# Expert stage: gathers and spreads as float32 matmuls in place of bfloat16 and float32r parts

## The chip, the cores and the metric

The kernel runs on one core of a Trainium2 chip. The metric is the device time of one execution in microseconds (us), as the median of several runs. Engines are named as in the profile: PE is TensorE (PEld its weight loads), DVE VectorE, ACT ScalarE, POOL GpSimd, SP SyncE, which issues most transfers.

## The reference, cut to what matters

One layer on 512 tokens of width 1024: a mixer (gated spatial MLP beside windowed attention), then a mixture of 32 experts, then a norm. The change lies in the mixture:

```python
glog = xf @ w_rg + b_rg                       # 4 groups
gsel = jnp.argmax(glog, axis=-1)
elog = jnp.take_along_axis(elog_all, gsel[:, None, None], axis=1)[:, 0]   # 8 experts of the group
topv, topi = lax.top_k(elog, 2)
tw = jax.nn.softmax(topv, axis=-1) * pg
...
for e in range(N_EXPERTS):
    h = jax.nn.silu(xf @ w_gate[e]) * (xf @ w_up[e])
    y = y + combine[:, e:e + 1] * (h @ w_down[e])
```

All inputs and the output are float32. `xf` is the normed `hn`, 512 x 1024. `w_gate[e]` and `w_up[e]` are 1024 x 512, `w_down[e]` is 512 x 1024. A token goes to two experts.

## The kernel before, in words

**Mixer** (to about 466 us). Projections are split by hand into float32r halves (hi and lo) and done with three matmuls each. Two places use plain float32 matmuls: the spatial gate (L627, stationary 128x128, 128 columns moving) and the attention scores (L565, 64 rows of contraction, 128 or 192 columns moving).

**Norm and routing** (about 466 to 502 us). ACT scales `hg` by the row's norm (`scale_h`, L923). Three bfloat16 parts of the normed rows are then made, tile by tile: ACT writes `hn_part[0]` (`first_part`, L927), POOL subtracts it in place (`first_rest`, L463), ACT writes `hn_part[1]` (`second_part`, L931), POOL subtracts again into `hn_part[2]` (`third_part`, L469). Beside it DVE computes the routing, a chain of small dependent instructions: the inverse root of the norm (L1004 to L1010), the group softmax's argument (L1268, for which ACT does an exponential at L946), the two best experts (L1261 to L1265), the softmax of two (L1284), and each token's row among the gathered rows. `make_onehot(i)` (L1306 to L1313) turns these into two weighted matrices for pair i, their sum `weight_a`, and the bfloat16 `onehot` (1 where the sum is over 0).

**Experts** (about 502 to 1017 us). A loop over 16 pairs of experts; each expert of a pair has 64 rows, so that a pair fills 128 partitions. The PE's order within pair i is written out by hand in `expert_pair`:

1. gate projection (L730, 16 matmuls; each uses 64 columns of the array, the two experts by turns), transposes of `weight_a` (L741), up projection (L730);
2. gather of the next pair's rows, tiles 0 and 1 of 8 (L714), transposes of the activations (L747), gather of tiles 2 and 3;
3. down projection in two halves of 512 columns (L755);
4. spread: for each half n and token block t, `onehotT` against `y_hi` and `y_lo` (L767, L768), added to `h_tok` by DVE (L1371);
5. gather of tiles 4 to 7.

A gather of one tile is, for 4 token blocks and 3 parts, a matmul of `hn_part[j]` (stationary) by `onehot` (moving, 128 columns): 12 bfloat16 matmuls accumulating exactly the float32 rows. The result goes through PSUM banks 2 and 3 to `packT` (ACT and DVE copy one half each). For the spread DVE sums each row's weight (L1353) and makes `onehotT` in float32r (L1354); ACT writes `y_hi` (the down result times the row's weight, in float32r, L970), and DVE `y_lo`, the rest (L1364).

A float32 matmul of 128 or more columns stands in the trace as two MATMUL instructions, each with its weight load; bfloat16 and float32r matmuls stand as one.

**Order of loads.** SP streams the weights through nine 16 KB buffers W[0] to W[8] (L333, L344, L376). Each load waits for the semaphore of the projection that used the buffer before. The load into W[8], which lies over `hg`, waits for `part2_ready`. ACT's order in routing is a fixed list of copies, scalings, parts and two exponentials.

**End.** After the last addition DVE sets `h_final`; ACT, DVE and POOL do the final norm, and SP stores the result.

## Time and profile before

| | |
|---|---|
| median of 3 runs | 1037.84 us (1035.43 to 1037.91) |
| profiled execution | span 1034.2 us from its first to its last instruction; no other time is printed for it |
| PE busy | 958.9 us, 93% |
| DVE, ACT, POOL busy | 489.2, 269.6, 25.0 us |
| moved by DMA | 247 MB, mean 239 GB/s |
| mean granted PE clock | 0.975 |

Busy time of an engine is the union of its instructions. A row of the timeline gives start, length, engine, line, operation, output <- input and a count of merged instructions. A row of a group gives busy time, mean length of one instruction, and the idle time in front with what ended it. Matmuls are pipelined: one's length is more than the distance to the next, so the pace is read from groups. L12 is line 12 of the kernel.

### The profile page before, as it was taken

To read this page: it belongs to the slowest core of one execution; us is meant where nothing else is said; L and a number is where in the kernel's file an instruction comes from. 1 tells how busy PE (TensorE), PEld (TensorE's weight loads), DVE (VectorE), ACT (ScalarE), POOL (GpSimd) and SP (SyncE) were. 2 spreads that over 40 slices of the span, in tenths; PEclk is the share of its full clock that TensorE was granted. 3 is DMA by queue.
4 is the path that set the end of the run, shared out by engine and by line. 5 is a ranking of instruction groups with operands and counts; after the bars stand their busy time and mean duration, and the time that the engine had idled before them with its cause. 6 is when DMAs were issued, how large, how long until landed. Compare 5 with 4: busy or idle time off the path is not lost.

```text
span 1034.2 us, 13947 instructions
## 1 busy us (share of the span) xinstructions
PE 958.9 (93%) x5675; PEld 624.5 (60%) x5675; DVE 489.2 (47%) x918; ACT 269.6 (26%) x427; POOL 25.0 (2%) x25
## 2 busy tenths in 40 slices
PE   3999999999999999593599999999999999999993
PEld 3888888777777888482454455554545545455442
DVE  3636335766672444258643443443443424434335
ACT  5323223644442211125121112120111211121102
POOL 0000000000000000005000000000000000000001
PEclk9999999999999999897699999999999999999997
DMA  8353222122115446834297999999999979999942
GB/s 285 82 111 93 86 78 82 42 82 71 52 57 138 132 120 229 282 127 163 107 364 323 387 395 388 413 402 390 394 383 413 402 268 392 412 387 395 396 155 83
DMA packets 93268, 247.12 MB, mean 239 GB/s; under 512 B 22168, under 2 KB 45744, under 8 KB 84784
## 3 DMA queue, kind: packets, MB, share of 16 engines
q1 hardware_dynamic: 90528, 245.90, 63.6%
q10 hardware_dynamic: 2704, 0.71, 0.3%
q8 instruction: 26, 0.43, 0.2%
q14 instruction: 10, 0.08, 0.0%
HBM read 244.50 MB, written 2.10 MB: 238 GB/s over the span
## 4 chain that ended last, share of the span: by engine, by line
PE 89%; DVE 6%; issue 1%; ACTq 1%; ACT 1%; DMA 1%; SPq 0%; DVEq 0%; POOL 0%; POOLq 0%
PE bank L730 22%; PE bank L755 11%; PE bank L714 9%; PE bank L504 9%; PE bank L506 9%; PE bank L505 9%; PE bank L767 3%; PE bank L768 3%; PE bank L531 3%; PE bank L533 3%; PE bank L532 2%; PE bank L565 2%; ACTq L900 1%; PE bank L741 1%; DMA x_tok<-x 1%
## 5 line engine op out<-in xcount | busy, mean ns | idle before, releaser
L730 PE MATMUL bank<-W,packT 128*64 128x512 f32 x1024 | 226.8, 595 | 2.9 <-issue 2.9
L730 PEld LDWEIGHTS bank<-W,packT 128*64 128x64 f32 x1024 | 74.1, 137 | 132.6 <-issue 131.6
L1017 DVE TENSOR_TENSOR wlo<-raw,whi 128x2048 fp32r<-128x2048 f32 x34 | 77.7, 2288 | 100.4 <-ACT whi L805 100.3
L504 PE MATMUL bank<-xnT_hi,whi 128*128 128x512 f32 x288 | 113.7, 395 | 0.8 <-DVE wlo L1017 0.8
L755 PE MATMUL bank<-W,actT 128*64 128x512 f32 x512 | 113.4, 595 | 0.0
L506 PE MATMUL bank<-xnT_hi,wlo 128*128 128x512 f32 x288 | 112.2, 390 | 0.0
L505 PE MATMUL bank<-xnT_lo,whi 128*128 128x512 f32 x288 | 112.2, 389 | 0.0
L714 PEld LDWEIGHTS bank<-onehot,hn_part 128*128 128x128 bf16 x1632 | 95.0, 99 | 25.0 <-issue 24.8
L714 PE MATMUL bank<-onehot,hn_part 128*128 128x128 bf16 x1632 | 101.9, 222 | 7.6 <-DVE onehot L1311 7.6
L1364 DVE SCALAR_TENSOR_TENSOR y_lo<-bank,small,y_hi 128x512 fp32r<-128x512 f32 x32 | 24.0, 751 | 145.4 <-ACT y_hi L970 145.4
L805 ACT ACTIVATE whi<-raw 128x2048 fp32r<-128x2048 f32 x34 | 64.8, 1909 | 87.5 <-PE bank L506 30.2
L1371 DVE TENSOR_TENSOR h_tok<-bank,h_tok 128x512 f32<-128x512 f32 x128 | 77.8, 678 | 0.0
L755 PEld LDWEIGHTS bank<-W,actT 128*64 128x64 f32 x512 | 35.3, 137 | 65.6 <-issue 64.0
L1353 DVE TENSOR_REDUCE small<-bank 128x1 f32<-128x512 f32 x16 | 11.1, 691 | 112.9 <-PE bank L741 112.9
L504 PEld LDWEIGHTS bank<-xnT_hi,whi 128*128 128x128 f32 x288 | 54.1, 188 | 12.6 <-issue 1.4
L506 PEld LDWEIGHTS bank<-xnT_hi,wlo 128*128 128x128 f32 x288 | 54.1, 188 | 11.4
L505 PEld LDWEIGHTS bank<-xnT_lo,whi 128*128 128x128 f32 x288 | 54.1, 188 | 10.8
L767 PE MATMUL bank<-y_hi,onehotT 128*128 128x512 f32 x128 | 51.8, 405 | 0.0
L970 ACT ACTIVATE y_hi<-bank,small 128x512 fp32r<-128x512 f32 x32 | 22.0, 688 | 113.3 <-PE bank L755 113.3
L963 ACT ACTIVATE silu_g<-bank 128x512 f32<-128x512 f32 x16 | 9.6, 597 | 156.6 <-PE bank L730 156.6
L768 PE MATMUL bank<-y_lo,onehotT 128*128 128x512 f32 x128 | 50.1, 391 | 0.0
L965 ACT ACTIVATE actT<-bank 128x512 f32<-128x512 f32 x16 | 9.6, 597 | 142.7 <-PE bank L747 142.7
(231 smaller groups left out, 1193.5 us busy)
## 6 DMA issues: line engine op xcount, KB each, us to landing
W<-w_up SPq DMA_DIRECT2D x32, 2048.0 KB, 11.2
W<-w_down SPq DMA_DIRECT2D x64, 1024.0 KB, 12.6
W<-w_gate SPq DMA_DIRECT2D x30, 2048.0 KB, 12.0
raw<-w_in SPq DMA_DIRECT2D x18, 1024.0 KB, 5.1
raw<-w_in SPq DMA_DIRECT2D x16, 256.0 KB, 4.4
raw<-w_branch_a SPq DMA_DIRECT2D x4, 1024.0 KB, 4.9
raw<-w_branch_b SPq DMA_DIRECT2D x16, 256.0 KB, 4.6
raw<-w_out SPq DMA_DIRECT2D x4, 1024.0 KB, 5.1
```

The source lines that it names most:

```text
L504: pe.matmul(dst, hi_w, hi_x, start=start, stop=False)
L505: pe.matmul(dst, hi_w, lo_x, start=False, stop=False)
L506: return pe.matmul(dst, lo_w, hi_x, start=False, stop=stop)
L531: pe.matmul(dst, xT_hi[:, kk, ts], w_h[:, k, :], start=first, stop=False)
L714: mm = pe.matmul(bank[2 + c // 4][:, (c % 4) * P:(c % 4 + 1) * P], hn_part[j][:, t, c, :], onehot[:, t, :], start=(t == 0 and j == 0), sto ...
L730: mm = pe.matmul(dst[s * ROWS:(s + 1) * ROWS, :], packT[:, c, s * ROWS:(s + 1) * ROWS], W[u][:, c * DE:(c + 1) * DE], start=(c == 0), stop ...
L755: mm = pe.matmul(bank[5 + n][s * ROWS:(s + 1) * ROWS, :], actT[:, c, s * ROWS:(s + 1) * ROWS], W[4 + s][:, c * D + n * 512:c * D + (n + 1) ...
L767: pe.matmul(dst, onehotT[:, t * P:(t + 1) * P], y_hi[:, n * 512:(n + 1) * 512], start=True, stop=False)
L768: pe.matmul(dst, onehotT[:, t * P:(t + 1) * P], y_lo[:, n * 512:(n + 1) * 512], start=False, stop=True).then_inc(spread_done, 1)
L805: act.activation(whi[c % 2][:, :], raw[c % 2][:, :], ACT.Copy).then_inc(hi_split, 1)
L1017: dve.tensor_tensor(wlo[c % 2][:, :], raw[c % 2][:, :], whi[c % 2][:, :].bitcast(F32), ALU.subtract).then_inc(lo_split, 1)
L1371: dve.tensor_tensor(part, bank[SPREAD_BANKS[n][t]][:, :], part, ALU.add).then_inc(h_added, 1)
```

## The change

The three bfloat16 parts become one float32 tensor `hn`, written by `scale_h` into its own place (it no longer overwrites `hg`). `first_part`, `second_part` and POOL's eight subtractions are gone. ACT scales all four tiles before its first exponential. `onehot` becomes float32 and is moved to another address. A gather is 4 float32 matmuls a tile in place of 12 bfloat16 ones. In the spread, the weights stay in the matrix: DVE copies the transposed `weight_a` to `weightT` (float32), ACT copies the down result to `y_rows` unweighted, and one float32 matmul takes the place of two float32r ones. `row_weight`, `onehotT`, `y_hi` and `y_lo` are gone. Two waits for `part2_ready` (SP's before W[8], PE's before the first gather) become waits for `hn_ready`.

```diff
--- before.py
+++ after.py
@@ -109,12 +97,11 @@
 
 
     W = [at(f"W{u}", [P, 8 * DE], F32, kb) for u, kb in enumerate((0, 16, 32, 48, 64, 80, 160, 144, 128))]
-    hn_part = [at(f"hn_part{j}", [P, TT, KT, P], BF16, 96 + 8 * j) for j in range(3)]
+    hn = at("hn", [P, TT, KT, P], F32, 96)
     packT = at("packT", [P, KT, P], F32, 120)
-    y_hi = at("y_hi", [P, D], F32R, 124)
+    y_rows = at("y_rows", [P, D], F32, 124)
     hg = at("hg", [P, TT, KT, P], F32, 128)
     hgT = [at(f"hgT{j}", [P, KT, 2 * P], F32, 144 + 8 * j) for j in range(2)]
-    hn_rest = hg
     h_tok = at("h_tok", [P, TT, D], F32, 176)
     ffn_g = at("ffn_g", [P, D], F32, 192)
     w_router = at("w_router", [P, KT, P // 2], F32, 196)
@@ -125,11 +112,10 @@
     silu_g = at("silu_g", [P, DE], F32, 200)
     act_rows = at("act_rows", [P, FT, P], F32, 202)
     actT = at("actT", [P, FT, P], F32, 204)
-    onehot = at("onehot", [P, TT, P], BF16, 206)
+    onehot = at("onehot", [P, TT, P], F32, 192)
     weight_a = at("weight_a", [P, TT, P], F32, 214)
     weight_b = at("weight_b", [P, TT, P], F32, 216)
-    y_lo = at("y_lo", [P, D], F32R, 192)
-    onehotT = at("onehotT", [P, SEQ], F32R, 196)
+    weightT = at("weightT", [P, SEQ], F32, 196)
     row_iota = at("row_iota", [P, P], F32, 207.5)
     final_g = at("final_g", [P, D], F32, 208)
     result = at("result", [P, TT, D], F32, 32)
@@ -146,7 +132,6 @@
     ln_stats, ln_mv = col(TT * 12), col(TT * 2)
     neg_max, sink_e, denom = ([col(REP) for _ in range(2)] for _ in range(3))
     w_first, w_second, row_first, row_second = col(TT), col(TT), col(TT), col(TT)
-    row_weight = col(1)
     half_sq = ln_stats[:, 0:2 * TT]
 
     room = [208.0]
@@ -264,8 +249,6 @@
         dve_step = sem("dve_step")
         hsq_summed, hg_ready, hgT_psum, hgT_a, hgT_b, rstd_ready = (
             sem(n) for n in ("hsq_summed", "hg_ready", "hgT_psum", "hgT_a", "hgT_b", "rstd_ready"))
-        part0_ready, rest_ready, part1_ready, part2_ready = (
-            sem(n) for n in ("part0_ready", "rest_ready", "part1_ready", "part2_ready"))
         logitsT_done, logitsT_ready, logits_turned = (
             sem(n) for n in ("logitsT_done", "logitsT_ready", "logits_turned"))
         route_sub, route_exp, picked_ready, ranks_done, routed = (
@@ -276,9 +259,8 @@
         gate_half_done = sem("gate_half_done")
         gate_done, up_done, silu_ready, rows_ready, rows_turned, actT_ready = (
             sem(n) for n in ("gate_done", "up_done", "silu_ready", "rows_ready", "rows_turned", "actT_ready"))
-        y_left, y_right, y_hi_ready, y_lo_ready = (sem(n) for n in ("y_left", "y_right", "y_hi_ready", "y_lo_ready"))
-        weights_turned, row_weight_ready, onehotT_ready = (
-            sem(n) for n in ("weights_turned", "row_weight_ready", "onehotT_ready"))
+        y_left, y_right, y_ready = (sem(n) for n in ("y_left", "y_right", "y_ready"))
+        weights_turned, weightT_ready = sem("weights_turned"), sem("weightT_ready")
         spread_done, h_added = sem("spread_done"), sem("h_added")
         ysq_summed, final_gained, out_stored = sem("ysq_summed"), sem("final_gained"), sem("out_stored")
         y_rstd_ready = sem("y_rstd_ready")
@@ -372,7 +354,7 @@
             sp.wait_ge(logitsT_done, 2)
             sp.dma_start(W[7][:, :], w_gate[0, 3].rearrange("(p c) n -> p (c n)", p=P)).then_inc(w_loaded[7], 16)
 
-            sp.wait_ge(part2_ready, TT)
+            sp.wait_ge(hn_ready, TT)
             sp.dma_start(W[8][:, :], w_up[0, 2].rearrange("(p c) n -> p (c n)", p=P)).then_inc(w_loaded[8], 16)
 
             for half, used in enumerate((gate_half_done, gate_done)):
@@ -457,23 +439,6 @@
             pool.wait_ge(route_iotas_made, 6)
             pool.affine_select(out=earlier[:, :], in_=all_ones[:, :], compare_op=ALU.is_gt, fill=0.0, base=0,
                                pattern=[[1, P]], channel_multiplier=-1).then_inc(route_iotas_made, 1)
-
-            def first_rest(t):
-                pool.wait_ge(part0_ready, t + 1)
-                pool.tensor_tensor(hn_rest[:, t, :, :], hn_rest[:, t, :, :], hn_part[0][:, t, :, :],
-                                   ALU.subtract).then_inc(rest_ready, 1)
-
-            def third_part(t):
-                pool.wait_ge(rest_ready, min(t + 2, TT))
-                pool.wait_ge(part1_ready, t + 1)
-                pool.tensor_tensor(hn_part[2][:, t, :, :], hn_rest[:, t, :, :], hn_part[1][:, t, :, :],
-                                   ALU.subtract).then_inc(part2_ready, 1)
-
-            first_rest(0)
-            for t in range(1, TT):
-                first_rest(t)
-                third_part(t - 1)
-            third_part(TT - 1)
 
             pool.wait_ge(late_loaded, 16 * 6)
             pool.wait_ge(h_final, 1)
@@ -710,10 +675,8 @@
                     if c == 0:
                         pe.wait_ge(onehot_ready, i + 1)
                     for t in range(TT):
-                        for j in range(3):
-                            mm = pe.matmul(bank[2 + c // 4][:, (c % 4) * P:(c % 4 + 1) * P],
-                                           hn_part[j][:, t, c, :], onehot[:, t, :],
-                                           start=(t == 0 and j == 0), stop=(t == TT - 1 and j == 2))
+                        mm = pe.matmul(bank[2 + c // 4][:, (c % 4) * P:(c % 4 + 1) * P], hn[:, t, c, :], onehot[:, t, :],
+                                       start=(t == 0), stop=(t == TT - 1))
                     if c % 4 == 3:
                         mm.then_inc(pack_done, 1)
 
@@ -757,20 +720,18 @@
                                            start=(c == 0), stop=(c == FT - 1))
                     mm.then_inc(done, 1)
 
-                pe.wait_ge(onehotT_ready, i + 1)
+                pe.wait_ge(weightT_ready, i + 1)
                 for n in range(2):
-                    pe.wait_ge(y_lo_ready, 2 * i + n + 1)
+                    pe.wait_ge(y_ready, 2 * i + n + 1)
                     for t in range(TT):
                         if n == 1 and t >= 2:
                             pe.wait_ge(h_added, 8 * i + t - 1)
-                        dst = bank[SPREAD_BANKS[n][t]][:, :]
-                        pe.matmul(dst, onehotT[:, t * P:(t + 1) * P], y_hi[:, n * 512:(n + 1) * 512], start=True, stop=False)
-                        pe.matmul(dst, onehotT[:, t * P:(t + 1) * P], y_lo[:, n * 512:(n + 1) * 512],
-                                  start=False, stop=True).then_inc(spread_done, 1)
+                        pe.matmul(bank[SPREAD_BANKS[n][t]][:, :], weightT[:, t * P:(t + 1) * P],
+                                  y_rows[:, n * 512:(n + 1) * 512], start=True, stop=True).then_inc(spread_done, 1)
                 gather_rows(i + 1, (4, 5, 6, 7))
                 pe.wait_ge(h_added, 8 * i + 8)
 
-            pe.wait_ge(part2_ready, TT)
+            pe.wait_ge(hn_ready, TT)
             pe.wait_ge(ranks_read, 1)
             gather_rows(0, range(KT))
             pe.wait_ge(counts_read, 1)
@@ -920,37 +881,21 @@
 
             def scale_h(t):
                 act.wait_ge(rstd_ready, t // 2 + 1)
-                act.activation(hn_rest[:, t, :, :], hg[:, t, :, :], ACT.Copy, scale=rstd[:, t:t + 1]).then_inc(hn_ready, 1)
-
-            def first_part(t):
-                act.wait_ge(hn_ready, t + 1)
-                act.activation(hn_part[0][:, t, :, :], hn_rest[:, t, :, :], ACT.Copy).then_inc(part0_ready, 1)
-
-            def second_part(t):
-                act.wait_ge(rest_ready, t + 1)
-                act.activation(hn_part[1][:, t, :, :], hn_rest[:, t, :, :], ACT.Copy).then_inc(part1_ready, 1)
+                act.activation(hn[:, t, :, :], hg[:, t, :, :], ACT.Copy, scale=rstd[:, t:t + 1]).then_inc(hn_ready, 1)
 
             copy_hgT(0)
             copy_hgT(1)
             scale_h(0)
-            first_part(0)
             square_h(1, TT - 1)
             scale_h(1)
             copy_hgT(2)
             copy_hgT(3)
-            first_part(1)
-            second_part(0)
             scale_h(2)
-            first_part(2)
+            scale_h(3)
             act.wait_ge(route_sub, 1)
             act.activation(gexp[:, :, :], gexp[:, :, :], ACT.Exp).then_inc(route_exp, 1)
-            second_part(1)
-            scale_h(3)
-            first_part(3)
-            second_part(2)
             act.wait_ge(route_sub, 2)
             act.activation(r4[5], r4[5], ACT.Exp).then_inc(route_exp, 1)
-            second_part(3)
 
             def copy_pack(i):
                 act.wait_ge(pack_done, 2 * i + 1)
@@ -964,11 +909,9 @@
                 act.wait_ge(rows_turned, i + 1)
                 act.activation(actT[:, :, :], bank[4][:, :].rearrange("p (c q) -> p c q", c=FT),
                                ACT.Copy).then_inc(actT_ready, 1)
-                act.wait_ge(row_weight_ready, i + 1)
                 for n, done in enumerate((y_left, y_right)):
                     act.wait_ge(done, i + 1)
-                    act.activation(y_hi[:, n * 512:(n + 1) * 512], bank[5 + n][:, :], ACT.Copy,
-                                   scale=row_weight).then_inc(y_hi_ready, 1)
+                    act.activation(y_rows[:, n * 512:(n + 1) * 512], bank[5 + n][:, :], ACT.Copy).then_inc(y_ready, 1)
 
             act.wait_ge(h_ready, 8)
             with act.Fori(0, PAIRS) as i:
@@ -1350,20 +1293,13 @@
                 copy_pack(i)
 
                 dve.wait_ge(weights_turned, i + 1)
-                dve.tensor_reduce(row_weight, bank[7][:, :], AX.X, ALU.add).then_inc(row_weight_ready, 1)
-                dve.tensor_scalar(onehotT[:, :], bank[7][:, :], 0.0, None, ALU.is_gt).then_inc(onehotT_ready, 1)
+                dve.tensor_copy(weightT[:, :], bank[7][:, :]).then_inc(weightT_ready, 1)
                 make_onehot(i + 1)
                 dve.wait_ge(silu_ready, i + 1)
                 dve.wait_ge(up_done, i + 1)
                 dve.tensor_tensor(act_rows[:, :, :].rearrange("q c p -> q p c"),
                                   silu_g[:, :].rearrange("q (p c) -> q p c", c=FT),
                                   bank[1][:, :].rearrange("q (p c) -> q p c", c=FT), ALU.mult).then_inc(rows_ready, 1)
-                dve.wait_ge(row_weight_ready, i + 1)
-                for n in range(2):
-                    dve.wait_ge(y_hi_ready, 2 * i + n + 1)
-                    dve.scalar_tensor_tensor(out=y_lo[:, n * 512:(n + 1) * 512], in0=bank[5 + n][:, :], scalar=row_weight,
-                                             in1=y_hi[:, n * 512:(n + 1) * 512].bitcast(F32), op0=ALU.mult,
-                                             op1=ALU.subtract).then_inc(y_lo_ready, 1)
                 for n in range(2):
                     for t in range(TT):
                         dve.wait_ge(spread_done, 8 * i + TT * n + t + 1)
```

## Rows read from the trace of the kernel before

**Rows 1.** The page: PE busy; DMA share in 40 slices, in tenths.
```profile
PE 958.9 (93%) x5675; PEld 624.5 (60%) x5675; DVE 489.2 (47%) x918; ACT 269.6 (26%) x427; POOL 25.0 (2%) x25
...
DMA  8353222122115446834297999999999979999942
```

**Rows 2.** Windows: length; PE, PEld, DVE, ACT, POOL busy; PEclk, DMA share, GB/s.
```profile
502.20:507.00 4.80, 4.72 (x45) 4.76 (x46) 4.21 (x24) 0.00 (x0) 0.00 (x0) 0.50 0.10 41
731.70:763.00 31.30, 31.30 (x216) 16.14 (x216) 12.62 (x26) 5.74 (x7) 0.00 (x0) 1.00 1.00 400
```

**Rows 3.** Waits of PE from 500 us on: total us, times, longest.
```profile
PE bank L714 <- DVE onehot L1311: 7.6, 1, 7.6
PE bank L730 <- issue: 2.9, 7, 0.5
```

**Rows 4.** The page's DMA issues: one load of an expert's matrix.
```profile
W<-w_up SPq DMA_DIRECT2D x32, 2048.0 KB, 11.2
```

**Rows 5.** Timeline of PE: start us, us; the first gather and the first projection.
```profile
502.27 7.91 PE L714 MATMUL bank<-onehot,hn_part 128*128 128x128 bf16 x96 [7.59 <-DVE onehot L1311]
510.12 7.09 PE L730 MATMUL bank<-W,packT 128*64 128x512 f32 x32
```

**Rows 6.** Groups by form on PE and its weight loads: busy us, mean ns.
```profile
L730 PE MATMUL bank<-W,packT 128*64 128x512 f32 x1024 | 226.8, 595 | 2.9 <-issue 2.9
...
L627 PE MATMUL bank<-wsT,v_tok 128*128 128x128 f32 x64 | 8.4, 274 | 0.0
...
L714 PEld LDWEIGHTS bank<-onehot,hn_part 128*128 128x128 bf16 x1632 | 95.0, 99 | 25.0 <-issue 24.8
...
L627 PEld LDWEIGHTS bank<-wsT,v_tok 128*128 128x128 f32 x64 | 8.3, 191 | 0.5
```

**Rows 7.** Timeline of PE, pair 0: first spread, last gather group, next projection.
```profile
535.01 0.50 PE L767 MATMUL bank<-y_hi,onehotT 128*128 128x512 f32 x1
...
538.77 2.85 PE L714 MATMUL bank<-onehot,hn_part 128*128 128x128 bf16 x48
541.56 0.65 PE L730 MATMUL bank<-W,packT 128*64 128x512 f32 x2
```

**Rows 8.** Timeline of PE: the float32 matmuls of the mixer.
```profile
145.99 1.05 PE L627 MATMUL bank<-wsT,v_tok 128*128 128x128 f32 x8
...
180.00 1.16 PE L565 MATMUL bank<-kT,qT 64*128 64x128 f32 x8
...
187.64 1.56 PE L565 MATMUL bank<-kT,qT 64*128 64x192 f32 x8
```

**Rows 9.** Timeline of the last pair: first spread, the eight additions.
```profile
1010.57 0.50 PE L767 MATMUL bank<-y_hi,onehotT 128*128 128x512 f32 x1
...
1012.08 4.86 DVE L1371 TENSOR_TENSOR h_tok<-bank,h_tok 128x512 f32<-128x512 f32 x8
```

**Rows 10.** Timeline of routing: GpSimd's subtraction, stalled and free VectorE instructions.
```profile
474.25 2.13 POOL L463 TENSOR_TENSOR hg<-hg,hn_part 128x1024 f32<-128x1024 f32 x1 [1.70 <-ACT hn_part L927]
474.41 1.98 DVE L1008 TENSOR_TENSOR small<-small 128x2 f32<-128x2 f32 x1
...
478.62 0.16 DVE L1008 TENSOR_TENSOR small<-small 128x2 f32<-128x2 f32 x1
...
481.74 2.06 DVE L1268 TENSOR_TENSOR gexp<-logits,route_t 128x16 f32<-128x16 f32 x1
...
492.49 0.28 DVE L1261 TENSOR_TENSOR route<-route,route_t 128x128 f32<-128x128 f32 x1
...
493.99 2.08 DVE L1284 TENSOR_SCALAR route_t<-route_t 128x4 f32<-128x4 f32 x1
```

**Rows 11.** Groups by form: ScalarE (465 to 503 us), VectorE (510 to 1018).
```profile
L923 ACT ACTIVATE hg<-hg,small 128x1024 f32<-128x1024 f32 x4 | 4.6, 1141 | 4.2 <-DVE small L1226 4.2
...
L1354 DVE TENSOR_SCALAR onehotT<-bank 128x512 fp32r<-128x512 f32 x16 | 10.9, 680 | 0.0
L1311 DVE TENSOR_SCALAR onehot<-weight_a 128x512 bf16<-128x512 f32 x16 | 6.8, 426 | 0.5
```

## The prediction

> **What bounds the kernel now.** I read the page first: TensorE (PE) is busy 93% of the span, and the row of DMA shares reads 9 of 10 over most of the second half [rows 1]. So two resources could bound the expert stage, which runs from 502 us to 1017 us. I then read the windows, one for each expert pair, and the chain of waits. In a steady pair PE is busy for all 31.30 us of a 31.30 us window at full clock, while the DMA share is 1.00 and 400 GB/s are moved [rows 2]. Which of the two is ahead is told by the waits: in the whole stage PE waits for a weight load never; its only waits are one for the first one-hot matrix and seven of at most 0.5 us at the loop's edge [rows 3]. A pair loads six matrices of 2,048 KB [rows 4], 12.6 MB, which at 400 GB/s take 31.5 us. PE sets the pace, and DMA would set it if PE became faster. So PE time added to a pair lengthens the kernel in full, and PE time taken away gains next to nothing.
>
> Ahead of the stage VectorE (DVE) is on the chain: PE stands idle until DVE has routed the tokens and written the first one-hot, at 502.27 us [rows 5].
>
> **Gathering.** Per pair, 96 bfloat16 matmuls become 32 float32 ones (8 tiles by 4 token blocks), and every float32 matmul is two MATMUL instructions: the spatial gate's 32 matmuls on L627 stand as x64 in the trace [rows 6]. So 96 instructions become 64. Now 48 of them take 538.77 to 541.56 [rows 7], 2.79 us or 0.058 each, 5.6 us a pair. The nearest row for the new shape is exact: L627 has float32, 128x128 stationary, 128 columns moving. Eight of its instructions take 1.05 us, and one takes 0.275 [rows 6, 8], so the step is (1.05 - 0.275)/7 = 0.111 us. 64 of these make 7.15, with 0.2 for the starts of three groups 7.35: **+1.8 us a pair**. Bounds: 0.107 (two cycles for each of 128 columns at 2.4 GHz) gives +1.5; the step of L565, (1.16 - 0.285)/7 = 0.125 [rows 8], gives +2.6.
>
> **Spreading.** Per pair, 16 float32r matmuls of 512 columns become 8 float32 ones, 16 instructions again. The old ones take 535.01 to 538.77 [rows 7], 3.76 us. For float32 with the full array and 512 columns there is no row, so the price must be bounded. The lower bound is L730: 32 instructions in 7.09 us, 0.214 each. The upper is the mean length of one of them less what every short one shows beyond its columns, 0.595 - 0.168 = 0.427 [rows 6]. These two rows disagree only if L730's instructions run one at a time. They use 64 columns of the array, alternately the left and right half, so two could run side by side, each 0.427 long. L565 decides, since its 128 and 192 column forms use all columns of the array and run one after the other: (1.56 - 0.322)/7 = 0.177 against 0.125, 0.052 us for 64 more columns, or 0.81 ns a column, which is two cycles of 2.4 GHz [rows 8]. So one instruction of 512 columns costs 0.427 us, 16 cost 6.83, with 0.15 for the start 6.98: **+3.2 us a pair**. With the lower bound it would be 3.6, that is -0.2; with L565's extra 0.018 us on each instruction it would be +3.5.
>
> The Trainium skill, in "FP8 and Floating Point Precision" (TensorE Precision Notes), says that true float32 goes through the array in four passes, which for 512 columns is an estimated 0.853 us a matmul and 6.8 us for the eight; taking L730's step at face value, it would be 3.4 us. L565's slope agrees with the page. "TensorE: Matmul & The Clock Gate" (Weight-path perf modes) adds that fast weight load is off for float32, and gives about P/1.2 ns, an estimated 107 ns, for 128 columns of weights: 64 loads would be a floor of 6.8 us for the gathers even if the matmuls were quicker. The trace agrees: weight loads take 191 ns on L627 and 99 ns on L714 [rows 6], and follow each other at the matmuls' step.
>
> **Sum for a pair.** +1.8 and +3.2 make +5.0 us. All of it lies on PE, which never waits now. DMA does not object: 12.6 MB in 36.7 us is 343 GB/s. Fifteen full pairs cost **+75.0 us**.
>
> **First and last.** The first gather runs at half clock until about 507 us (0.50 from 502.20 to 507.00 [rows 2]) and takes 7.85 us, from 502.27 to 510.12 [rows 5]. If the clock rises as late after its start, the float32 form does 4.9/0.214 = 23 instructions at half speed and 41 at 0.111, 9.6 us with the start: **+1.8**. In the last pair half of a pair's gathers lie ahead of the end (+0.9), and the other half behind the spread that nobody waits for. The end there is DVE's last addition: now spread at 1010.57, additions until 1012.08 + 4.86 = 1016.94 [rows 9], 6.4 us. DVE will now keep up with PE (0.61 us an addition against 0.86 between two spreads), so the last one ends at 6.98 + 0.2 + 0.69 = 7.9 us after the spread's start: +1.5. Together **+2.4**.
>
> **Routing.** The eight GpSimd subtractions of some 2.1 us go. A DVE instruction that starts on SBUF operands while one runs ends only with it: L1008 on 128x2 values lasts 1.98 us beside the subtraction at 474.25, and 0.16 three instructions later with GpSimd quiet [rows 10]. There are seven such instructions on DVE's chain, the first 1.98 and the last 2.08 long [rows 10]; against their twins of the same shape (0.16 for a few values, 0.28 for 128x128 [rows 10]) they lose 12.5 us in all. These are L1008, L1010, L1268, L1261, L1262, L1265 and L1284, and all lie in front of the one-hot. **-12.4**, since a little of one stall hides PE's ranks. What is late next is DVE's own chain without them. ScalarE's two exponentials now stand behind the scaling of tiles 2 and 3, 1.14 us each [rows 11], released at about 475.6 (the root's memset of 479.2 less two stalls, 3.6); they end by 478, and the first exponential, asked for after L1268, now from 481.74 [rows 10], is wanted at 481.74 - 3.6 + 0.2 = 478.3. Its reader comes 10 us later, so even a 2 us lateness is covered. If stalls stayed, it would be 0; nothing suggests a loss.
>
> **Edits with no cost.** SP's load into W[8] waits for hn_ready (some 478) rather than part2_ready (496): it then finds idle transfer engines (4 and 2 tenths in the slices from 465 to 517 us [rows 1]), its buffer hg is read for the last time by then, and the waits queued behind it on SP (gate_half_done) come after pair 0's start in any case. DVE drops a reduction, a one-hot and two y_lo a pair for one copy; PE waits for none of them in the stage [rows 3], so their going gains nothing. What PE now waits for is one ScalarE copy of 0.7 us a half; the right half's has the first four spreads, 3.4 us, as its cover, and would cost 0.7 us a pair without it. Writing the one-hot as float32 costs nothing to 0.25 us (L1354 writes 512 four-byte values in 0.680, L1311 512 two-byte ones in 0.426 [rows 11]), and is on the chain once (**+0.2**). No wait is added that an earlier one did not already hold.
>
> **Total.** 1034.2 + 75.0 + 1.8 + 2.4 + 0.2 - 12.4 = 1101.2 us of span. No time is printed for the profiled execution alone; the span is 3.6 us below the median of the three runs, 1037.84, and I take that as what lies around it: **1104.8 us**, or 6.5% slower. This measurement can tell some 0.3% from no change.
>
> **Rivals.**
> *Float32 streams one column a cycle.* Then L730's step holds for every shape. If the gathers' weight loads also hid, they would take 64 x 0.056 + 0.2 = 3.8 us (-1.8) and the spread -0.2, so PE alone would need 29.7 us a pair. DMA would take over at its 31.5 us, and what is left is the routing and about 2 us at the pairs' edges and the ends: 1034.2 - 12.4 - 2 + 3.6 = 1023 us, faster than before. It decides if the slope per column is 0.42 ns instead of 0.81; L730 speaks for it, L565 against. Chance 0.03.
> *The same for the spread alone,* with the gathers held by weight loads at 0.111: a pair costs +1.8 - 0.2 = +1.6, fifteen 24.0, the first gather and the last pair's +2.7, the routing -12.2: 1034.2 + 14.5 + 3.6 = 1052 us. Chance 0.04.
> *Weight loads are not hidden* at 32 gathers in a row and cost their 0.188: 64 x 0.188 + 0.2 = 12.2, +6.6 a pair instead of +1.8: 1104.8 + 15 x 4.8 + 4 = 1181 us. L627 has just 8 in a row and shows no sign of it. Chance 0.03.
> *The stalls have another cause* and stay: 1104.8 + 12.4 = 1117 us. Chance 0.04.
> *The change does what it says,* as in the forecast: 0.86.
>
> **Range.** Low ends: gather +1.5, spread +3.1, 15 x 0.4 = 6 less, and 2 to 3 of slack in the clock and the routing: 1096. High ends: gather +2.2 (between L627 and L565, nearer to L627), spread +3.5, 15 x 0.7 = 10.5 more: 1115. I give 1095 to 1115, which leaves out the first three rivals and the tail of the fourth. Faster by over 0.3%: 0.03; within: 0.01; slower: 0.96.
>
> **What would show it.** Right: gathers as x1088 float32 instructions (17 x 64) 0.111 apart and 275 ns long; spreads 0.427 apart; pair windows of 36.7 us with PE busy throughout and DMA share near 0.86; the DVE instructions named above back at 0.16 to 0.29 us, and the first gather at about 490 us. Wrong: pair windows still 31.5 us with DMA share 1.0 (first rival), or gaps in PE before a spread or a gather, named by a wait for DVE, ScalarE or a weight buffer.

## The result, and the profile after

The changed kernel takes 1100.37 us (median of 4 runs, 1099.82 to 1100.58) against 1036.78 us before: a ratio of 1.061, interval 1.060 to 1.063. Forecast were 1104.8 us in a range of 1095 to 1115. The profiled execution took 1099.82 us with a span of 1098.1, 63.9 more than the span of before.

The page of the kernel after: engines and DMA shares, as in [rows 1].

```profile
PE 1040.3 (95%) x5131; PEld 655.0 (60%) x5131; DVE 455.6 (41%) x870; ACT 259.1 (24%) x419; POOL 7.9 (1%) x17
...
DMA  7443221221136368356598889888988698889821
```

A window of one pair in the middle of the expert stage (length; PE, PEld, DVE, ACT, POOL busy; PEclk, DMA share, GB/s), as in [rows 2]:

```profile
718.70:755.18 36.48, 36.48 (x185) 17.82 (x184) 11.29 (x23) 5.55 (x7) 0.00 (x0) 1.00 0.87 345
```

PE is busy for the whole of it at full clock, and the DMA share has fallen from 1.00 to 0.87. So PE set the pace before and sets it now; only the margin to the transfers has grown. The waits of PE from 485 us on are down to one, the first one-hot; the seven short ones of [rows 3] are gone:

```profile
PE bank L678 <- DVE onehot L1254: 5.7, 1, 5.7
```

Groups by form (busy us, mean ns), as in [rows 6], first PE, then its weight loads:

```profile
L678 PE MATMUL bank<-onehot,hn 128*128 128x128 f32 x1088 | 133.5, 280 | 5.7 <-DVE onehot L1254 5.7
L729 PE MATMUL bank<-y_rows,weightT 128*128 128x512 f32 x256 | 114.1, 599 | 0.0
```

```profile
L678 PEld LDWEIGHTS bank<-onehot,hn 128*128 128x128 f32 x1088 | 128.9, 195 | 26.4 <-issue 26.4
```

The gather is 1088 instructions of 280 ns, the spread 256 of 599. (The float32 transposes, L741 and L747 in the kernel before, stand as one instruction each, x4 for four of them; only the matmuls proper stand as two.) The timeline of PE shows the first gather and projection, and then pair 0 with its gathers (L678), down projection (L718), spread (L729) and the next pair's first projection (L693), as in [rows 5, 7]:

```profile
490.17 9.72 PE L678 MATMUL bank<-onehot,hn 128*128 128x128 f32 x64 [5.68 <-DVE onehot L1254]
499.82 7.09 PE L693 MATMUL bank<-W,packT 128*64 128x512 f32 x32
...
514.45 2.05 PE L678 MATMUL bank<-onehot,hn 128*128 128x128 f32 x16
...
516.77 1.95 PE L678 MATMUL bank<-onehot,hn 128*128 128x128 f32 x16
518.65 7.09 PE L718 MATMUL bank<-W,actT 128*64 128x512 f32 x32
525.67 7.13 PE L729 MATMUL bank<-y_rows,weightT 128*128 128x512 f32 x16
532.64 3.73 PE L678 MATMUL bank<-onehot,hn 128*128 128x128 f32 x32
536.30 7.09 PE L693 MATMUL bank<-W,packT 128*64 128x512 f32 x32
```

Starts give the prices. Gathers: 516.34 less 514.45 (the transposes follow at 516.34), 518.65 less 516.77 and 536.30 less 532.64 are 1.89 + 1.88 + 3.66 = 7.43 us, in the longest group 0.114 an instruction; 16 spread instructions take 532.64 - 525.67 = 6.97 us, 0.436 each.

The timeline of the routing, answering to [rows 10]; L951, L953, L1211, L1204 and L1227 are what was L1008, L1010, L1268, L1261 and L1284:

```profile
474.21 0.16 DVE L951 TENSOR_TENSOR small<-small 128x2 f32<-128x2 f32 x1
...
474.60 0.16 DVE L953 SCALAR_TENSOR_TENSOR small<-small 128x2 f32<-128x2 f32 x1
...
478.50 0.17 DVE L1211 TENSOR_TENSOR gexp<-logits,route_t 128x16 f32<-128x16 f32 x1
...
480.27 0.29 DVE L1204 TENSOR_TENSOR route<-route,route_t 128x128 f32<-128x128 f32 x1
...
483.80 0.16 DVE L1227 TENSOR_SCALAR route_t<-route_t 128x4 f32<-128x4 f32 x1
...
489.60 0.43 DVE L1254 TENSOR_SCALAR onehot<-weight_a 128x512 f32<-128x512 f32 x1
```

None of the seven that were long before is above 0.29 us (L1205 and L1208, once L1262 and L1265, take 0.29 each). The one-hot in float32 takes 0.43 us, as much as the bfloat16 one did. The last pair's spread, the gather behind it and the last addition, as in [rows 9]:

```profile
1072.87 7.13 PE L729 MATMUL bank<-y_rows,weightT 128*128 128x512 f32 x16
...
1079.84 3.73 PE L678 MATMUL bank<-onehot,hn 128*128 128x128 f32 x32
1080.04 0.69 DVE L1307 TENSOR_TENSOR h_tok<-bank,h_tok 128x512 f32<-128x512 f32 x1 [0.17 <-PE bank L729]
```

The account of the 63.9 us, from these starts and those of before:

| stretch | before | after | difference | forecast |
|---|---|---|---|---|
| start of the first gather | 502.27 | 490.17 | -12.1 | -12.2 |
| first gather | 7.85 | 9.65 | +1.8 | +1.8 |
| 15 pairs, first to last gate projection | 475.56 (985.68 - 510.12) | 547.20 (1047.02 - 499.82) | +71.6 | +75.0 |
| from there to the end | 48.5 | 51.1 | +2.6 | +2.4 |

Three of four terms are within 0.2 us. The pairs are off by 3.4 us, and the forecast of 67.0 us for the whole span was 3.1 too high. The other 1.3 us between 1104.8 and 1100.4 lie outside the span: the prediction added 3.6 us to the span for the median time, and it was 1100.37 - 1098.1 = 2.3.

### The profile page after: what moved, and what is told of

Its sections match the earlier page's. It is cut to its first block, busy times and chain, and to the rows that moved or that the text cites. A ratio compares the mean times of both kernels' runs of the same rounds, so it can differ in the third digit from the quotient of the medians.

```text
span 1098.1 us, 12759 instructions
## 1 busy us (share of the span) xinstructions
PE 1040.3 (95%) x5131; PEld 655.0 (60%) x5131; DVE 455.6 (41%) x870; ACT 259.1 (24%) x419; POOL 7.9 (1%) x17
## 4 chain that ended last, share of the span: by engine, by line
PE 91%; DVE 4%; ACTq 1%; ACT 1%; issue 1%; DMA 1%; SPq 0%; DVEq 0%; POOL 0%; POOLq 0%
PE bank L693 20%; PE bank L678 11%; PE bank L729 10%; PE bank L718 10%; PE bank L469 8%; PE bank L470 8%; PE bank L471 8%; PE bank L496 2%; PE bank L497 2%; PE bank L498 2%; PE bank L530 2%; ACTq L861 1%; DMA x_tok<-x 1%; PE bank L704 1%; PE bank L559 1%
## 5 line engine op out<-in xcount | busy, mean ns | idle before, releaser
L693 PE MATMUL bank<-W,packT 128*64 128x512 f32 x1024 | 226.8, 595 | 0.0
L1307 DVE TENSOR_TENSOR h_tok<-bank,h_tok 128x512 f32<-128x512 f32 x128 | 88.6, 692 | 196.4 <-PE bank L729 196.4
L693 PEld LDWEIGHTS bank<-W,packT 128*64 128x64 f32 x1024 | 70.7, 137 | 132.5 <-issue 130.6
L678 PEld LDWEIGHTS bank<-onehot,hn 128*128 128x128 f32 x1088 | 128.9, 195 | 26.4 <-issue 26.4
L678 PE MATMUL bank<-onehot,hn 128*128 128x128 f32 x1088 | 133.5, 280 | 5.7 <-DVE onehot L1254 5.7
L960 DVE TENSOR_TENSOR wlo<-raw,whi 128x2048 fp32r<-128x2048 f32 x34 | 77.7, 2288 | 100.1 <-ACT whi L766 100.0
L729 PE MATMUL bank<-y_rows,weightT 128*128 128x512 f32 x256 | 114.1, 599 | 0.0
L718 PE MATMUL bank<-W,actT 128*64 128x512 f32 x512 | 113.4, 595 | 0.0
L729 PEld LDWEIGHTS bank<-y_rows,weightT 128*128 128x128 f32 x256 | 47.3, 190 | 66.6 <-issue 66.6
L718 PEld LDWEIGHTS bank<-W,actT 128*64 128x64 f32 x512 | 35.3, 137 | 65.9 <-issue 64.0
L1296 DVE COPY weightT<-bank 128x512 f32<-128x512 f32 x16 | 11.1, 692 | 110.6 <-PE bank L704 110.6
L914 ACT ACTIVATE y_rows<-bank 128x512 f32<-128x512 f32 x32 | 19.1, 597 | 121.9 <-PE bank L718 121.9
L1300 DVE TENSOR_TENSOR act_rows<-silu_g,bank 128x512 f32<-128x512 f32 x16 | 16.9, 1057 | 48.8 <-PE bank L693 48.8
## 6 DMA issues: line engine op xcount, KB each, us to landing
W<-w_down SPq DMA_DIRECT2D x64, 1024.0 KB, 11.5
W<-w_gate SPq DMA_DIRECT2D x30, 2048.0 KB, 12.1
```

What stands on the lines that cost most here:

```text
L678: mm = pe.matmul(bank[2 + c // 4][:, (c % 4) * P:(c % 4 + 1) * P], hn[:, t, c, :], onehot[:, t, :], start=(t == 0), stop=(t == TT - 1))
L693: mm = pe.matmul(dst[s * ROWS:(s + 1) * ROWS, :], packT[:, c, s * ROWS:(s + 1) * ROWS], W[u][:, c * DE:(c + 1) * DE], start=(c == 0), stop ...
L718: mm = pe.matmul(bank[5 + n][s * ROWS:(s + 1) * ROWS, :], actT[:, c, s * ROWS:(s + 1) * ROWS], W[4 + s][:, c * D + n * 512:c * D + (n + 1) ...
L729: pe.matmul(bank[SPREAD_BANKS[n][t]][:, :], weightT[:, t * P:(t + 1) * P], y_rows[:, n * 512:(n + 1) * 512], start=True, stop=True).then_i ...
L960: dve.tensor_tensor(wlo[c % 2][:, :], raw[c % 2][:, :], whi[c % 2][:, :].bitcast(F32), ALU.subtract).then_inc(lo_split, 1)
L1307: dve.tensor_tensor(part, bank[SPREAD_BANKS[n][t]][:, :], part, ALU.add).then_inc(h_added, 1)
```

## The experiments

Times are medians, and each is set against runs of the kernel before on the same chip, whose median lay between 1036.2 and 1037.1 us.

**One half of the change at a time.** First the gathers alone:

```diff
-    hn_part = [at(f"hn_part{j}", [P, TT, KT, P], BF16, 96 + 8 * j) for j in range(3)]
-    onehot = at("onehot", [P, TT, P], BF16, 206)
+    hn = at("hn", [P, TT, KT, P], F32, 96)
+    onehot = at("onehot", [P, TT, P], F32, 112)
...
-                        for j in range(3):
-                            mm = pe.matmul(..., hn_part[j][:, t, c, :], onehot[:, t, :], ...)
+                        mm = pe.matmul(..., hn[:, t, c, :], onehot[:, t, :], ...)
```

> The kernel before with the gather half of the change alone: one float32 tensor of normed rows, float32 gathers, no bfloat16 parts and no GpSimd subtractions; the spread keeps its float32r halves. Theory (PE sets the pace, a float32 instruction costs two cycles a column): a pair goes from 31.44 us of PE work to 33.3 (+1.85), the routing loses its 12 us of stalls, the first gather costs 1.8 more. If the 0.5 us that a pair at the loop's edge loses now comes from transfers that are late (DMA at its limit), it is gone here too: 1036.8 - 12.1 + 1.8 + 15 x 1.57 + 0.9 = 1051 us. If it comes from PE's instruction stream it stays: 1054 us. Rival (the spread's price and the gather's price only add up through a shared limit): anything under 1045 us.

Measured: 1051.0 us, ratio 1.014 (1.013 to 1.016). Then the spread alone (the changed kernel's L1296, L914 and L729 in the kernel before):

> The kernel before with the spread half alone: weights left in the matrix, one float32 matmul for each of the eight blocks, no y_hi and y_lo; gathers in three bfloat16 parts and GpSimd's subtractions stay. Theory: a pair goes from 31.44 to 34.65 us (+3.2), the stalls of the routing stay, the last addition ends 1.5 us later: 1036.8 + 15 x 2.92 + 1.5 = 1082 us with the loop's edge gone, 1086 us with it there. With the first gather at 7.9 us as before. The effects of this run and of the gather alone, added, should give the whole change (+63.6 us). Rival (float32 at one cycle a column with the whole array): 1036 us.

Measured: 1083.2 us, ratio 1.046 (1.044 to 1.048). One pair of each, gathers alone and then spread alone, in windows cut from one gate projection's start to the next:

```profile
567.88:601.16 33.28, 33.28 (x186) 17.77 (x185) 12.63 (x26) 5.74 (x7) 0.00 (x0) 1.00 0.95 376
```

```profile
580.00:614.64 34.64, 34.64 (x218) 15.91 (x217) 11.28 (x23) 5.55 (x7) 0.00 (x0) 1.00 0.91 362
```

33.28 and 34.64 us, both as forecast from the 31.44 of pair 0 before. So the two prices stand for themselves: +1.84 for the gathers, +3.20 for the spread. The whole-array float32 price, which had no row before, is the upper of the two bounds. The two runs also show something that the prediction did not have. In the kernel before, pairs in the loop take 31.5 and 32.0 us by turns, the longer ones with a gap at the loop's edge; in both halves all pairs are alike, and the gaps are gone. Each half therefore ends the gaps on its own account: from the first to the last gate projection they are 23.5 us (1000.44 - 501.34 less 475.56) and 44.0 us (1030.25 - 510.73 less 475.56) longer, 67.5 together, 4.1 less than the 71.6 of the whole change, and the gaps are worth 15 x 0.26 = 3.9. The medians, +14.8 and +47.0 = 61.8 against 63.6, show only about half of that, as the mixer ended 1.8 and 1.6 us later in the profiles of the two halves than in that of the kernel before; why, no run shows.

**The stalls of the routing.** The subtractions were cut down to one element (the third part and most of the subtraction are left out of the result):

```diff
-                pool.tensor_tensor(hn_rest[:, t, :, :], hn_rest[:, t, :, :], hn_part[0][:, t, :, :],
+                pool.tensor_tensor(hn_rest[0:1, t, 0, 0:1], hn_rest[0:1, t, 0, 0:1], hn_part[0][0:1, t, 0, 0:1],
...
-                                           hn_part[j][:, t, c, :], onehot[:, t, :],
+                                           hn_part[min(j, 1)][:, t, c, :], onehot[:, t, :],
```

> The kernel before with GpSimd's eight subtractions cut from 128x1024 elements to one element each; the gather reads the second part twice in place of the third, so that the third part and most of the subtraction are left out of the result, with the same number of matmuls. Theory (the seven long VectorE instructions wait for GpSimd): all of them fall to 0.16 to 0.29 us, the first gather starts 12.4 us earlier, 1024.4 us. Rival (the long instructions have another cause, as ScalarE's writes beside them or a wait on a semaphore): they stay and so does the time, 1036.8 us.

Measured: 1024.7 us, ratio 0.989 (0.988 to 0.991). The timeline of its routing, with the same lines as before:

```profile
475.27 0.19 POOL L463 TENSOR_TENSOR hg<-hg,hn_part 1x1 f32<-1x1 f32 x1 [3.66 <-ACT hn_part L927]
475.44 0.16 DVE L1008 TENSOR_TENSOR small<-small 128x2 f32<-128x2 f32 x1
...
479.15 0.17 DVE L1268 TENSOR_TENSOR gexp<-logits,route_t 128x16 f32<-128x16 f32 x1
...
484.44 0.16 DVE L1284 TENSOR_SCALAR route_t<-route_t 128x4 f32<-128x4 f32 x1
```

ScalarE still writes both parts beside them, so ScalarE is not the cause. And the other way round, on a spare buffer that no other engine reads or waits for, eight subtractions put back into the changed kernel:

```diff
+            pool.wait_ge(hn_ready, 2)
+            for n in range(8):
+                pool.tensor_tensor(spare[:, 0:1024], spare[:, 0:1024], spare[:, 1024:2048], ALU.subtract).then_inc(spare_cleared, 1)
+                pool.wait_ge(spare_cleared, n + 2)
```

> The changed kernel with eight GpSimd subtractions of 128x1024 float32 put back beside the routing, on a spare buffer that nobody reads, one after the other from the second scaled tile on. Theory (a GpSimd instruction that reads SBUF holds up VectorE instructions that take two SBUF inputs or copy fast from SBUF): about eight VectorE instructions of the routing last some 2 us again, and the time is 1100.4 + 12 to 14 = 1113 us. Rival: no change, 1100.4 us.

Measured: 1113.3 us, 12.9 above the changed kernel; the first gather starts at 503.30, 13.1 later. Its timeline has the subtractions in one row of eight, and VectorE's instructions on two values a row waiting for the end of each:

```profile
471.92 19.32 POOL L449 TENSOR_TENSOR spare<-spare 128x1024 f32<-128x1024 f32 x8 [0.47 <-ACT hn L893]
...
474.53 2.19 DVE L957 TENSOR_SCALAR small<-small 128x2 int32<-128x2 int32 x1
...
476.95 2.19 DVE L961 SCALAR_TENSOR_TENSOR small<-small 128x2 f32<-128x2 f32 x1
```

With memsets in their place (`pool.memset(spare[:, :], 1.0)`):

> As the run with eight subtractions put back, but with eight GpSimd memsets of 128x2048 float32, which write and read nothing, about 2.1 us each. If only a GpSimd instruction that reads SBUF holds up VectorE's two-input instructions, just the single-input ones in their fast mode (tensor_scalar, copy from SBUF) can be stretched here, of which few lie in the routing: +0 to +4 us, 1100 to 1104 us. If any GpSimd instruction does, the same as with the subtractions: 1113 us.

Measured: 1104.7 us (1103.0 to 1105.8).

```profile
473.85 14.84 POOL L449 MEMSET spare<- 128x2048 f32 x8 [0.44 <-ACT hn L893]
...
475.81 1.73 DVE L956 TENSOR_SCALAR small<-small 128x2 f32<-128x2 f32 x1
477.57 1.83 DVE L957 TENSOR_SCALAR small<-small 128x2 int32<-128x2 int32 x1
...
479.43 0.16 DVE L960 TENSOR_TENSOR small<-small 128x2 f32<-128x2 f32 x1
```

Beside 14.84 us of memsets two instructions are held, both `tensor_scalar` with a single input, for 1.73 and 1.83 us. The two-input L960 behind them runs in 0.16, as do all the other two-input ones. That is +3.2 us. The median is 4.3 above the changed kernel and the profiled execution (1105.5) 5.7; of that some 2 us were there before the first memset began, as the mixer was already that much late (VectorE's addition of 466.09 stands at 468.09). The Trainium skill ("SBUF — State Buffer", section "SBUF: two separate sides") says that VectorE's two-input instructions are locked out only by a GpSimd instruction that reads SBUF, and single-input ones in a two-port mode by any. The two runs agree. A later `tensor_scalar` (L1222, on 128x16 values, 0.17 us from 484.89) is no counterexample: the memset beside it, one of 1.80 us, ended at about 484.96, so there was next to nothing to wait for. Beside a subtraction a reduction, which has one input, is not held either: in the kernel before, L1264 takes 0.29 us from 489.57, while GpSimd subtracts from 489.47 for 2.12. The prediction's rule, that any VectorE instruction on SBUF operands ends only with the subtraction, is too wide by that.

**What holds the gather's pace.** Rows and one-hot in float32r, in the changed kernel (the gathered rows lose the low bits):

```diff
-    hn = at("hn", [P, TT, KT, P], F32, 96)
-    onehot = at("onehot", [P, TT, P], F32, 192)
+    hn = at("hn", [P, TT, KT, P], F32R, 96)
+    onehot = at("onehot", [P, TT, P], F32R, 192)
```

> The changed kernel with the normed rows and the one-hot in float32r: each gather matmul is one instruction and not two, 128 columns with four-byte weights; the gathered rows lose the bits that float32r leaves out. Separates what holds the gather's 0.114 us an instruction. Theory A (two cycles for each column; a weight load of 128 four-byte columns takes as long, so both are at the limit): the instruction stays at 0.107 to 0.114 us because of its weight load, a pair's gather costs 3.8 us in place of 7.4, pair 32.9 us, 1100.4 - 15 x 3.6 - 4 = 1042 us. Theory B (weight loads are no limit): 0.056 us, gather 2.0 us, PE needs 31.1 us a pair and the transfers their 31.5: about 1022 us.

Measured: 1049.1 us, pair 33.2 us. Timeline of PE, second and third group of gathers in pair 0, and the group of the weight loads:

```profile
515.82 1.09 PE L678 MATMUL bank<-onehot,hn 128*128 128x128 f32 x8
516.84 7.09 PE L718 MATMUL bank<-W,actT 128*64 128x512 f32 x32
...
530.43 2.30 PE L678 MATMUL bank<-onehot,hn 128*128 128x128 f32 x16
532.65 7.09 PE L693 MATMUL bank<-W,packT 128*64 128x512 f32 x32
```

```profile
L678 PEld LDWEIGHTS bank<-onehot,hn 128*128 128x128 f32 x544 | 69.0, 200 | 26.4 <-issue 26.4
```

Each matmul is one instruction now, but it is no shorter: 8 in 516.84 - 515.82 = 1.02 us (0.128 each), 16 in 2.22 us (0.139 each), with weight loads of 200 ns. Theory B's 0.056 us is out: halving the instructions of a gather does not bring their pace down to what the columns alone would take. The weight load is the likely limit, as theory A has it, but that is not shown: the pace is above A's 0.107 to 0.114, and for plain float32 columns and weight load would give the same 0.107, so no run tells them apart. Theory A was 7 us too low. The fifteen pairs are 6.7 us longer than it had them: 15 x 0.32 = 4.8 us, as a pair takes 33.20 and not 32.88 (slower instructions, and a wait of PE of 0.22 us for VectorE's product of the activations), and 1.9 us in pair 0 alone, whose first projection takes 8.95 us (497.53 to 506.48) and not 7.02, because the granted clock is still 0.50 until about 501. An estimate from these steps: two float32r parts would take 2 x 0.128 = 0.26 us where the three bfloat16 ones take 3 x 0.058 = 0.17.

**Can the 12 us be had without the change?** The first pair gathers in float32 from the rows as they are, and the subtractions come behind the first one-hot:

```diff
+            pool.wait_ge(onehot_ready, 1)
+            for pair in range(2):
+                for job in (first_rest, third_part):
+                    job(2 * pair)
+                    job(2 * pair + 1)
```

> The kernel before, with the first pair's gather alone in float32 from the normed rows as they are, and GpSimd's eight subtractions moved behind the first one-hot, so that they run beside the first gather and the first two projections (into two small buffers, not in place). All later gathers keep the bfloat16 parts, the spread its float32r halves. Nothing is left out of the computation. Theory: the routing loses its stalls (-12.1), the first gather costs +1.8 at half clock, pairs stay as they were: 1036.8 - 10.3 = 1026.5 us. GpSimd now stalls VectorE where it writes the second one-hot, which PE asks for at about 514 us; if that came late it would show as a wait of PE on the one-hot, up to +3 us. Rival (the stalls are worth less than their sum, because the expert stage is held by transfers that do not start earlier): pairs get longer and 1033 us or more is left.

Measured: 1037.5 us, ratio 1.000 (1.000 to 1.001): nothing. The first gather did start at 490.1 us. Its timeline after that:

```profile
490.07 4.21 POOL L468 TENSOR_TENSOR rest<-hg,hn_part 128x1024 f32<-128x1024 f32 x2 [74.31 <-DVE onehot L1327]
...
492.34 1.99 DVE L1346 TENSOR_TENSOR route_e<-route_e 128x31 f32<-128x31 f32 x1
...
496.51 1.99 DVE L1345 COPY route_e<-route_e 128x4 f32<-128x4 f32 x1
...
511.21 0.69 DVE L1334 COPY packT<-bank 128x512 f32<-128x512 f32 x1
...
511.95 5.36 PE L735 MATMUL bank<-W,packT 128*64 128x512 f32 x16 [8.56 <-DVE packT L1334]
```

The stalls moved with the subtractions. VectorE counts the overflow rows there, another chain of small instructions, which was stretched from 7 to 21 us; the copy of the gathered rows stands behind it in VectorE's order, and PE waited 8.56 us for that. Theory and rival both missed this; the rival's 1033 us or more came true for another reason, since the pairs behind the first take 31.5 and 32.0 us by turns as before. So the subtractions were put behind the count, and ScalarE's copy of the first gathered half ahead of its second parts. The first of the two edits:

```diff
-            pool.wait_ge(onehot_ready, 1)
+            pool.wait_ge(routed, 1)
```

> As the run with the parts made later, but GpSimd starts its eight subtractions only when VectorE has counted the overflow rows (some 497 us), and ScalarE copies the first gathered half ahead of the second parts. Nothing is left out of the computation. In the run before, GpSimd stretched that count from 7 to 21 us, and PE waited 8.6 us for the copy of the gathered rows behind it. Theory: this wait is gone, the subtractions take 497.5 to about 515 us, PE asks for the parts at about 514.5 and waits up to 2 us: 1036.8 - 12.1 + 1.8 + 1 to 2 = 1028 us. Rival (the expert stage is held by the transfers, which start no earlier): PE waits for weights somewhere in the pairs and 1033 us or more is left.

Measured: 1030.1 us, ratio 0.992 (0.991 to 0.994). Waits of PE from 480 us on (L706 belongs to the routing, L785 is the first gather, L735 a gate projection, L719 a later gather):

```profile
PE bank L706 <- DVE picked L1294: 7.0, 1, 7.0
PE bank L785 <- DVE onehot L1325: 5.7, 1, 5.7
PE bank L735 <- issue: 3.0, 7, 0.5
PE bank L719 <- DVE onehot L1325: 2.1, 1, 2.1
```

The 8.6 us wait is gone, and one of 2.1 us for the second one-hot is there, made beside the last subtractions, just above the 2 us that were allowed for it. PE waits for no weights, so the rival is out. The run is 2 us above its forecast: in this profile the mixer ends 2.3 us later than in that of the kernel before (VectorE's last copy before the norm at 474.97 against 472.63), and the five times lie from 1028.2 to 1031.0.

**The gap at the loop's edge.** In the kernel before, every second pair of the loop took 0.5 us more, with a gap in front of the next pair's first projection. The loop's body holds two pairs, and the gaps stand at its edges: six of some 0.46 us at the jumps back, and one of 0.21 where the loop is entered. Its timeline at one of them:

```profile
631.16 4.86 DVE L1371 TENSOR_TENSOR h_tok<-bank,h_tok 128x512 f32<-128x512 f32 x8
...
633.44 2.85 PE L714 MATMUL bank<-onehot,hn_part 128*128 128x128 bf16 x48
...
636.76 4.51 PE L730 MATMUL bank<-W,packT 128*64 128x512 f32 x20 [0.46 <-issue]
```

The first guess was late transfers, as the DMA share stood at 1.00; the expectation of the gathers alone had even named the gap's end as a sign of them, and the gap did end there. The test leaves half of each down matrix unloaded from the third expert on, so that the sums over experts are not the reference's:

```diff
+                        some = FT if used is None else 2
...
-                                     .rearrange("a (p c) n -> p a c n", p=P)).then_inc(w_loaded[4 + n], 16)
+                                     .rearrange("a (p c) n -> p a c n", p=P)[:, :, 0:some, :]).then_inc(w_loaded[4 + n], 16)
```

> The kernel before, with half of each down projection's matrix left unloaded from the third expert on (what lay there is used again, so the sums over experts are not the reference's); PE's work and every other instruction are the same. Bytes a pair fall from 12.6 to 10.5 MB. Tests what the 0.5 us is that PE loses in front of every second pair of the kernel before, and that is in none of the kernels whose pair takes 33 us or more. Theory (the transfers, at their limit, are late there): all pairs take 31.44 us and the time falls by 4 to 5 us, to 1032.3 us. Rival (the loop's edge, PE's own instruction stream): 1036.8 us with the seven gaps as before.

Measured: 1036.6 us, ratio 0.999 (0.999 to 1.000). A window of it, and its wait at the gate projection:

```profile
573.00:605.00 32.00, 32.00 (x220) 16.06 (x218) 12.93 (x27) 5.74 (x7) 0.00 (x0) 1.00 0.82 328
```

```profile
PE bank L731 <- issue: 3.1, 7, 0.6
```

The DMA share is down to 0.82 and the seven gaps are as before: it was not the transfers, and the end of the gaps in the slower kernels had another reason. A candidate is in the rows above: VectorE's last addition ends at 631.16 + 4.86 = 636.02, just ahead of the gather's end (633.44 + 2.79 = 636.23), and PE waits for it right before the loop's jump. The same wait stands between the two pairs of the body, where there is no jump, and costs nothing: there the gather takes 2.80 us to the next projection (665.46 to 668.26) and the addition ends 0.2 us ahead as well. In the changed kernel the gather has 2.8 us to run after the last addition (in the last pair, 1080.73 to 1083.5). So the wait was moved past the edge:

```diff
                 gather_rows(i + 1, (4, 5, 6, 7))
-                pe.wait_ge(h_added, 8 * i + 8)
...
+                if not (isinstance(i, int) and i == 0):
+                    pe.wait_ge(h_added, 8 * i)
                 project(gate, bank[0], gate_done, packed=i + 1, half_done=half_done)
```

> The kernel before, with PE's wait for VectorE's eight additions moved from the end of a pair to the start of the next, so past the loop's edge (each pair but the first waits for the additions of the pair before). Nothing is left out. Theory: in the kernel before, the last addition ends only some 0.2 us ahead of the last gather (572.81 against 573.00), PE's sequencer cannot run ahead over that wait, and the jump behind it costs about 0.5 us that nothing covers; in kernels with a slow spread the gather covers it. With the wait past the edge the seven gaps are gone, all pairs take 31.44 us, and the time falls by 3 to 5 us, to 1032 to 1034 us. Rival (the edge costs PE's instruction stream this time wherever the wait stands): seven gaps as before, 1037 us.

Measured: 1034.2 us, ratio 0.998 (0.997 to 0.999). The same place:

```profile
631.25 4.87 DVE L1372 TENSOR_TENSOR h_tok<-bank,h_tok 128x512 f32<-128x512 f32 x8
...
633.50 2.85 PE L714 MATMUL bank<-onehot,hn_part 128*128 128x128 bf16 x48
636.45 4.94 PE L730 MATMUL bank<-W,packT 128*64 128x512 f32 x22
```

From gather to projection it is 2.95 us, where it was 3.32, and 2.79 where no edge lies between; no gap is reported any more. So most of the gap belongs to the wait in front of the jump. 0.16 us of each edge stays: the longer pairs take 31.60 us in place of 31.98 and the one at the loop's entry 31.61 in place of 31.71, 2.4 us in all, which is why the gain was 2.2 us and not 3 to 5. That PE's sequencer cannot run ahead over the wait is the explanation offered; no run shows it directly.

**A version that beats both.** The last two edits together:

> The parts made after the overflow count, together with the wait moved past the edge. Nothing is left out. Theory: the two gains add up, 1030.1 - 3 to 5 = 1025 to 1027 us. Rival: as the parts alone, 1030 us; or, once pairs take 31.44 us, transfers at 400 GB/s (31.5 us for 12.6 MB) begin to hold PE and leave 1028 us or more.

Measured: 1026.6 us, ratio 0.990 (0.989 to 0.992) to the kernel before, and 73.8 us below the changed one. The two gains, measured one by one as 7.0 and 2.2 us, make 9.2, and together they are 9.8: they add up within what medians of a few runs can tell. (The forecast was met although the 3 to 5 us in it did not come true.) Pairs take 31.5 and 31.6 us by turns, and PE waits for no weights. It computes all that the reference does, with the three exact parts.

## Why the prediction was right, and where it was off

- **Who sets the pace.** Right. A pair takes 36.48 us, where 36.7 was forecast. PE was busy throughout before and after, and the DMA share fell to 0.87, where 0.86 was forecast. The run with fewer bytes moved nothing, so the transfers had no share in the time before, though their engines were as good as full.
- **Gathers, +1.8 a pair.** Right: 7.43 for 5.58 us, +1.85, from an instruction of the same shape in another stage (L627). The step is 0.114 against 0.111. (Sixty-four steps of 0.111 make 7.10 us and not the 7.15 of the prediction, which changes nothing.) Its remark that the trace agrees with an estimate of 107 ns a weight load says too much: loads are 191 ns long on L627 and 195 on L678, the distance between them is that of the matmuls, and with float32r it is 0.128.
- **Spread, +3.2 a pair.** Right: 6.97 for 3.76 us, +3.21. The choice between 0.214 and 0.427 us, made by the slope of L565, held. (It used 0.322 us for the instructions of 192 columns, the median of both forms; their own mean is 0.336, which gives 0.78 ns a column and the same choice.) That L730 runs two instructions side by side in the two halves of the array fits: its instructions are as long as the spread's, 595 against 599 ns, at half the step, 0.219 against 0.436 us. The two rivals that rested on it (1023 and 1052 us) are refuted by the 599 ns and 0.436 us steps of the spread.
- **Pairs together, +75.0: the mis-sized term.** It measured +71.6. The two prices add up to 5.06 us, but the pair before was not 31.44 us on average: it was 475.56/15 = 31.70, with 0.5 us at each jump of the loop. The prediction read the seven short waits and left them out of the sum, as if they would stay. A slower gather or a slower spread covers them, as the two half changes show; with only the wait moved, most of them goes too.
- **Routing, -12.4.** Right in cause, as the one-element subtractions and the subtractions put back show (1024.7 against 1036.2 us, -11.5, with the first gather at 490.8 in its profile; and +12.9). The term of +0.2 for a float32 one-hot was not needed: it takes 0.43 us as before, and the mixer's end was 0.4 us later in this profile.
- **First gather and last pair, +1.8 and +2.4.** +1.8 and +2.6. The first had some luck: the prediction let the clock rise as late after the gather's start as before, and it did (0.50 from 490.17 to 495.00, 0.97 in the microsecond behind). But the old first gather, 7.85 us in the profile before, took 6.73, 6.76 and 6.88 us in three runs that leave it alone (the moved wait, fewer bytes, the spread alone), where the clock rose sooner after its start.
- **Around the span, +3.6.** Measured 2.3, so 1.3 us of the 4.4 that the forecast was too high. In the profiled execution after, whose own time is printed, 1099.82 - 1098.1 = 1.7 us lie around the span; the rest of the 3.6 will have been the distance of the profiled execution before from its median, for which no time is printed.
- **Weight loads not hidden (1181 us)** is refuted: steps of 0.114 us with loads of 195 ns, so successive loads overlap. **Stalls with another cause (1117 us)** is refuted by the changed kernel itself and by two runs, subtractions of one element and subtractions put back.
- **What kept the error small** is that the one cost with no row had two rows that disagreed by a factor of two, and a third that decided between them. Had L730's step been taken at its face for the spread, the forecast would have been 1052 us, 48 too low.

## What to carry to other kernels

Price a matmul from an instruction with the same type, columns of weights and columns moved, and where the array is used by halves, take the length of one instruction, less what short ones show beyond their columns, and not the distance between two. A GpSimd instruction that reads SBUF beside a chain of small VectorE instructions can cost that chain nearly the whole of its own length (here 19.3 us of subtractions cost 13.1, and 14.8 us of memsets 3.2); move it, and look first at what VectorE does where it lands. When a gap goes away together with a resource's load, that does not make the resource its cause: change the load alone. Short waits that a trace books as "issue" belong in the sum too: ask which later instruction would cover them.

## What the runs showed of the hardware that was not expected

- A GpSimd memset holds up single-input `tensor_scalar` instructions on VectorE (1.73 and 1.83 us for 0.17) and no two-input ones, while a GpSimd subtraction holds up both (2.19 us), but not a reduction (0.29 us).
- A float32r matmul of 128 columns with 128 columns of weights takes 0.128 to 0.139 us, more than one of float32's two instructions (0.114), though at 512 columns it takes 0.235 (3.76/16) against 0.436. What sets the pace at 128 columns stays open.
- A wait of PE on a semaphore right in front of a loop's jump costs up to 0.5 us even when it is fulfilled 0.2 us before PE's work runs out; the same wait behind the jump leaves 0.16. Which part of PE's front end this is stays open.
- With transfers at a DMA share of 1.00 and 400 GB/s, 17% fewer bytes changed the time by less than can be measured.
